# The way down of a mixture's turned block, moved between the two halves of the gate and the value products

## The chip, the cores and the metric

The kernel runs on one core of a Trainium2 chip. The metric is the device time of one execution in microseconds (us); the time before is the median of three runs.

## The reference, cut to what matters

The whole program is two transformer blocks on 256 tokens of width 1024: a convolution block and an attention block, then a second block with band attention and an RWKV mixer. Two of its layers are mixtures of experts, and only they are touched. Both compute, for every expert e, a gated product:

```python
# first mixture: 8 experts of width 3584, two for each token
y = y + gates[..., e:e + 1] * ((silu(h @ w13[e][:, :F]) * (h @ w13[e][:, F:])) @ w2[e])
# second mixture: 32 experts of width 256
h = silu(xt @ e_gate[e]) * (xt @ e_up[e])
out = out + (h * comb[:, e:e + 1]) @ e_down[e]
```

## The kernel before, in words

**Steps and units.** Each mixture gathers the tokens of every expert into 128 slots and then runs N steps. The first (m1) has 56 steps, 7 for each expert; the second (m2) has 16, two for each group of four experts. A step handles 512 hidden columns. It has two gate products (gate weights times tokens, half of the 1024 inputs each: `up(n, 0)` and `up(n, 1)`, into a gate bank), two value products (`up(n, 2)`, `up(n, 3)`, into a value bank), four transposes of the hidden block (`turn`) and two products back to width 1024 (`down`, into banks 5 and 6). Each of the six products eats one unit of weights: 1 MB, brought by two transfers of 512 KB, and 12 matmuls of 512 columns.

**The chain of one block.** ScalarE makes silu of the gate bank (line 1412). VectorE multiplies it by the value bank (`hidden`, line 1649), which needs the end of `up(n, 3)`. TensorE turns the result in the next step (`turn(n - 1)`, line 1291). ScalarE copies the turned block as its high part `mh_hi` (line 1416), VectorE makes the rest `mh_lo` (line 1654), and `down(n - 1)` (lines 1311 to 1315) needs both. After an expert's last `down` the banks 5 and 6 are emptied (lines 1422 and 1660).

**Rings.** A unit lands in `ring_raw` (6 slots). ScalarE writes its high part to `ring_hi` (line 1389) and VectorE the rest to `ring_lo` (line 1396); both rings have 3 slots. A high copy of unit i waits until TensorE has finished unit i - 3, the rest waits for the high copy, and TensorE needs both. SyncE starts the transfer of unit i once unit i - 6 has been split.

**Order.** It is written out by hand for each engine. `Moe.unit(n, what)` says which place in the list of units each product of step n has, and everything goes by this list: the transfers, the splits, and the count `unit_done`, which TensorE raises after each unit. Before, the six units that TensorE goes through from one step's start are gate 0, gate 1, value 2, value 3 of step n and the two of `down(n - 1)`; their places are base to base + 5, with base = `unit(n, 0)`. ScalarE's order in a step, with `hi(i)` for a high copy, is: hi(base+3), the copy of the turned block, hi(base+4), silu, hi(base+5) to hi(base+8). VectorE's order is: lo(base+3), the rest of the turned block, lo(base+4), lo(base+5), `hidden(n)`, lo(base+6), lo(base+7), and after an expert's end the emptying of the banks, lo(base+8).

Of the kernel before, what the change touches and what calls it, by code (L numbers as in the profile page):

```python
# [89 lines left out]
class Moe:  # L90
# [10 lines left out]

    def unit(self, n, what):

        if what < 4:
            return what if n == 0 else 6 * n - 2 + what
        return 6 * n + what + (4 if n < self.N - 1 else 0)


def col_rows():
# [13 lines left out]
def block_pair(nc, A, out, known):  # L123
# [134 lines left out]
    with ExitStack() as ctx:  # L258
# [939 lines left out]
        def moe_pe(pe, m, H, counted=None):  # L1198
# [62 lines left out]
            def halves(i):  # L1261
                eng.wait_ge(T.sem("hi_done"), SB + i + 1)
                eng.wait_ge(T.sem("lo_done"), SB + i + 1)
                s = (SB + i) % SPLIT
                return ring_hi[:, s, :], ring_lo[:, s, :]

            def finish(last, i, label):
                last.then_inc(T.sem("unit_done"), 1)
                T.mark(label, "unit_done", U + i + 1)

            def up(n, what, o):
                g, h, i = n // m.per, what % 2, m.unit(n, what)
                if m.G == 1:
                    by_k = lambda w: (lambda k: w.rearrange("p (k n) -> p k n", n=512)[:, k, :])
                else:
                    by_k = lambda w: (lambda k: w.rearrange("p (e k n) -> p e k n", e=2, k=4)[:, :, k, :])
                    o = o.rearrange("p (e n) -> p e n", e=2)
                wh, wl = (by_k(w) for w in halves(i))
                for k in range(4):
                    kk = 4 * h + k  # L1280
                    mm(o, xg_hi[:, g, kk, :], wh(k), start=(kk == 0), stop=False)  # L1281
                    mm(o, xg_lo[:, g, kk, :], wh(k), start=False, stop=False)  # L1282
                    last = mm(o, xg_hi[:, g, kk, :], wl(k), start=False, stop=(kk == KT - 1))  # L1283
                finish(last, i, f"{nm} up {n} {what}")

            def turn(n):
                eng.wait_ge(*T.at(f"{nm} hidden {n}"))
                if n:
                    eng.wait_ge(*T.at(f"{nm} turned_lo {n - 1}"))
                for k in range(4):  # L1290
                    last = nc.tensor.transpose(bank[TURN][:, k * P:(k + 1) * P], hid[n % 2][:, k * P:(k + 1) * P],  # L1291
                                               ident[:, :])
                last.then_inc(pe.tick(f"mm {nm} turn {n}"), 1)

            def down(n):
                g, first = n // m.per, n % m.per == 0
                eng.wait_ge(*T.at(f"{nm} turned_lo {n}"))
                if first and g:
                    eng.wait_ge(*T.at(f"{nm} y {g - 1}"))
                if n == 0:  # L1300
                    eng.wait_ge(*T.at(f"{nm} selT 0"))
                    eng.wait_ge(*T.at(f"{nm} selT 1"))
                for h in range(2):
                    i = m.unit(n, 4 + h)
                    wh, wl = (w.rearrange("p (k n) -> p k n", n=D) for w in halves(i))
                    for c in range(2):
                        o, ns = bank[DOWN + c][:, :], slice(512 * c, 512 * c + 512)
                        for k in range(2):
                            begin = first and h == 0 and k == 0
                            end = n % m.per == m.per - 1 and h == 1 and k == 1  # L1310
                            mm(o, mh_hi[:, 2 * h + k, :], wh[:, k, ns], start=begin, stop=False,  # L1311
                               skip_group_check=True)
                            mm(o, mh_lo[:, 2 * h + k, :], wh[:, k, ns], start=False, stop=False,  # L1313
                               skip_group_check=True)
                            last = mm(o, mh_hi[:, 2 * h + k, :], wl[:, k, ns], start=False, stop=end,  # L1315
                                      skip_group_check=True)
                    finish(last, i, f"{nm} down {n}")

            def gate_slots():
                eng.wait_ge(*T.at(f"{nm} gates"))  # L1320
                for g in range(m.NG):
                    for a in range(TT):
                        last = mm(bank[SPARE][:, g * m.G:(g + 1) * m.G], psel[:, a, g * P:(g + 1) * P].bitcast(F32),
                                  gates[:, g, a, 0:m.G], start=(a == 0), stop=(a == 1))
                last.then_inc(pe.tick(f"mm {nm} ge"), 1)

            def turn_sel(q):
                if q == 2:
                    eng.wait_ge(*T.at(f"{nm} ge"))
                if q == 3:  # L1330
                    eng.wait_ge(*T.at(f"{nm} selT 2"))
                for i in range(2):
                    for a in range(TT):
                        last = nc.tensor.transpose(bank[turn_bank[q]][:, i * S + a * P:i * S + a * P + P],
                                                   psel[:, a, (2 * q + i) * P:(2 * q + i + 1) * P].bitcast(F32),
                                                   ident[:, :])
                last.then_inc(pe.tick(f"mm {nm} selT {q}"), 1)
# [12 lines left out]
            for n in range(m.N):  # L1350
                if n >= 2:
                    eng.wait_ge(*T.at(f"{nm} silu {n - 2}"))
                up(n, 0, bank[gate_bank(n)][:, :])
                if n:
                    turn(n - 1)
                up(n, 1, bank[gate_bank(n)][:, :])
                if n >= 2:
                    eng.wait_ge(*T.at(f"{nm} hidden {n - 2}"))
                up(n, 2, bank[value_bank(n)][:, :])
                up(n, 3, bank[value_bank(n)][:, :])  # L1360
                if n == 0:
                    gate_slots()
                    turn_sel(0)
                    turn_sel(1)
                if n in (1, 2):
                    turn_sel(n + 1)
                    T.mark(f"{nm} psel read", *pe.last)
                if n:
                    down(n - 1)
            eng.wait_ge(*T.at(f"{nm} selT 3"))  # L1370
            for g in range(m.NG - 1):
                if g == m.NG - 2:
# [785 lines left out]
        def _(eng):  # L2158
# [299 lines left out]
            def last_rows():  # L2458
                turn_row(turned)
                turn_row(turned)  # L2460

            moe_pe(pe, m1, tD, last_rows)
            rest_pe(pe, m1, tD)
            ln_stats("ln3", tA, 26, 16)
# [36 lines left out]
            ln_stats("ln5", tA, 0, 16, summed=True)  # L2501
            pe.stage = "m2"
            moe_pe(pe, m2, xT)
            rest_pe(pe, m2, xT)
            ln_stats("ln6", tA, 18, 0)
# [754 lines left out]
```

## Time and profile before

| | |
|---|---|
| median of 3 runs | 2320.7 us (2320.04 to 2328.55) |
| the profiled execution's own time | 2317.63 us |
| its span | 2315.9 us |
| TensorE busy in the span | 2225.8 us |
| VectorE busy in the span | 1719.8 us |
| ScalarE busy in the span | 1378.0 us |
| steps of m1 and m2 | 56 and 16, one every 17.0 us |

The span is the profiled execution from first to last instruction; 1.7 us of its time lie around it. In the timeline each row has a start, a duration, the engine, the line, the operation, output and inputs, and in brackets how long the engine had been idle and what ended that. A matmul's duration includes its way through the array, so rows overlap; what one costs in a dense stream is the distance between starts. PEld is TensorE's load of stationary operands.

### The profile page before, as it was taken

How to read it: one execution, taken by the hardware profiler on the slowest of the kernel's cores; microseconds unless marked ns; L12 is line 12 of the kernel's file. 1: busy time of each engine (PE TensorE's matmuls, PEld its weight loads, DVE VectorE, ACT ScalarE, POOL GpSimd, SP SyncE). 2: the span in 40 equal slices, each digit the busy share in tenths (PEclk: the TensorE clock that was granted, in tenths of full speed). 3: DMA queues.
4: the chain of work that ended last, by engine and by line, in shares of the span. 5: the costliest groups of instructions: out<-in, count | busy, mean ns of one | idle time of the engine just before them, and what ended most of it. 6: DMA issues, size and time to landing. Idle time of an engine off the chain costs nothing.

```text
span 2315.9 us, 36497 instructions
## 1 busy us (share of the span) xinstructions
PE 2225.8 (96%) x14806; PEld 1910.1 (82%) x14806; DVE 1719.8 (74%) x1680; ACT 1378.0 (60%) x1296; POOL 88.3 (4%) x164
## 2 busy tenths in 40 slices
PE   7999999998999999999999999998998897999997
PEld 6778999887788888888888888887997796888887
DVE  3865444656789888888888888875586467899954
ACT  3244334545677777777777777764564335777743
POOL 7400000001000000000000000000000000000000
PEclk9999999999999999999999999999999899999999
DMA  9785754676599999999999999995640232999930
GB/s 334 231 276 185 255 184 164 205 232 200 189 344 393 376 366 376 367 376 369 372 370 372 373 368 372 370 347 41 199 143 8 93 128 92 374 369 367 375 116 19
DMA packets 339968, 618.80 MB, mean 267 GB/s; under 512 B 24813, under 2 KB 165944, under 8 KB 339800
## 3 DMA queue, kind: packets, MB, share of 16 engines
q1 hardware_dynamic: 338992, 616.13, 76.2%
q8 instruction: 121, 1.98, 0.4%
q10 hardware_dynamic: 808, 0.30, 0.1%
q14 instruction: 47, 0.39, 0.0%
HBM read 614.26 MB, written 1.05 MB: 266 GB/s over the span
## 4 chain that ended last, share of the span: by engine, by line
PE 75%; DVE 3%; ACT 2%; issue 1%; DVEq 0%; ACTq 0%
PE bank L1281 11%; PE bank L1282 11%; PE bank L1283 11%; PE bank L1313 6%; PE bank L1315 6%; PE bank L1311 6%; PE bank L2191 4%; PE bank L2192 4%; PE bank L2193 4%; PE bank L1254 1%; PE bank L1291 1%; PE bank L600 1%; PE bank L1345 1%; PE bank L2284 1%; PE bank L2275 1%
## 5 line engine op out<-in xcount | busy, mean ns | idle before, releaser
L1396 DVE TENSOR_TENSOR ring_lo<-ring_raw,ring_hi 128x2048 fp32r<-128x2048 f32 x432 | 988.2, 2291 | 137.9 <-ACT ring_hi L1389 137.5
L1389 ACT ACTIVATE ring_hi<-ring_raw 128x2048 fp32r<-128x2048 f32 x432 | 827.8, 1920 | 297.4 <-PE bank L1283 181.3
L1281 PE MATMUL bank<-ring_hi,xg_hi 128*128 128x512 f32 x1152 | 456.3, 396 | 5.8 <-DVE ring_lo L1396 3.6
L1282 PE MATMUL bank<-ring_hi,xg_lo 128*128 128x512 f32 x1152 | 449.6, 390 | 0.0
L1283 PE MATMUL bank<-ring_lo,xg_hi 128*128 128x512 f32 x1152 | 449.4, 390 | 0.0
L2191 PE MATMUL bank<-Hh,ring_hi 128*128 128x256 f32 x1032 | 298.9, 290 | 13.4 <-DVE Hl L2890 7.9
L476 DVE TENSOR_TENSOR ring_lo<-ring_raw,ring_hi 128x2048 fp32r<-128x2048 f32 (+1 forms) x96 | 217.8, 2280 | 124.7 <-ACT ring_hi L458 117.3
L2193 PE MATMUL bank<-Hh,ring_lo 128*128 128x256 f32 x1032 | 294.9, 286 | 0.0
L2192 PE MATMUL bank<-Hl,ring_hi 128*128 128x256 f32 x1000 | 286.1, 286 | 0.0
L1281 PEld LDWEIGHTS bank<-ring_hi,xg_hi 128*128 128x128 f32 x1152 | 216.4, 188 | 51.3 <-ACT ring_hi L1389 4.0
L1283 PEld LDWEIGHTS bank<-ring_lo,xg_hi 128*128 128x128 f32 x1152 | 216.3, 188 | 46.8
L1282 PEld LDWEIGHTS bank<-ring_hi,xg_lo 128*128 128x128 f32 x1152 | 216.5, 188 | 43.1
L458 ACT ACTIVATE ring_hi<-ring_raw 128x2048 fp32r<-128x2048 f32 (+1 forms) x96 | 181.6, 1899 | 79.8 <-PE bank L2193 55.0
L1311 PE MATMUL bank<-ring_hi,mh 128*128 128x512 f32 x576 | 228.4, 396 | 0.0
L1313 PE MATMUL bank<-ring_hi,mh 128*128 128x512 f32 x576 | 228.2, 396 | 0.0
L1315 PE MATMUL bank<-ring_lo,mh 128*128 128x512 f32 x576 | 228.1, 396 | 0.0
L2191 PEld LDWEIGHTS bank<-Hh,ring_hi 128*128 128x128 f32 x1032 | 201.0, 195 | 18.3 <-issue 14.0
L2193 PEld LDWEIGHTS bank<-Hh,ring_lo 128*128 128x128 f32 x1032 | 201.4, 195 | 0.0
L2192 PEld LDWEIGHTS bank<-Hl,ring_hi 128*128 128x128 f32 x1000 | 195.5, 196 | 0.1
L1315 PEld LDWEIGHTS bank<-ring_lo,mh 128*128 128x128 f32 x576 | 108.4, 188 | 26.2
L1313 PEld LDWEIGHTS bank<-ring_hi,mh 128*128 128x128 f32 x576 | 108.5, 188 | 25.8
L1311 PEld LDWEIGHTS bank<-ring_hi,mh 128*128 128x128 f32 x576 | 108.4, 188 | 25.7
(496 smaller groups left out, 2751.3 us busy)
## 6 DMA issues: line engine op xcount, KB each, us to landing
ring_raw<-in_moe_w SPq DMA_DIRECT2D x672, 512.0 KB, 5.1
ring_raw<-in_ada_w SPq DMA_DIRECT2D x96, 512.0 KB, 5.4
ring_raw<-in_ffn_w SPq DMA_DIRECT2D x66, 512.0 KB, 5.0
ring_raw<-in_exp_gate SPq DMA_DIRECT2D x64, 512.0 KB, 4.7
ring_raw<-in_exp_up SPq DMA_DIRECT2D x64, 512.0 KB, 4.8
ring_raw<-in_exp_down SPq DMA_DIRECT2D x64, 512.0 KB, 4.7
ring_raw<-in_w_in SPq DMA_DIRECT2D x42, 512.0 KB, 5.0
ring_raw<-in_conv_in_w SPq DMA_DIRECT2D x16, 512.0 KB, 8.8
```

Of the source, the lines that this page charges most:

```text
L476: nc.vector.tensor_tensor(ring_lo[:, i % SPLIT, 0:kt * c], ring_raw[:, n % RAW, 0:kt * c], ring_hi[:, i % SPLIT, 0:kt * c].bitcast(F32), A ...
L1281: mm(o, xg_hi[:, g, kk, :], wh(k), start=(kk == 0), stop=False)
L1282: mm(o, xg_lo[:, g, kk, :], wh(k), start=False, stop=False)
L1283: last = mm(o, xg_hi[:, g, kk, :], wl(k), start=False, stop=(kk == KT - 1))
L1311: mm(o, mh_hi[:, 2 * h + k, :], wh[:, k, ns], start=begin, stop=False, skip_group_check=True)
L1313: mm(o, mh_lo[:, 2 * h + k, :], wh[:, k, ns], start=False, stop=False, skip_group_check=True)
L1315: last = mm(o, mh_hi[:, 2 * h + k, :], wl[:, k, ns], start=False, stop=end, skip_group_check=True)
L1389: nc.scalar.activation(ring_hi[:, at % SPLIT, :], ring_raw[:, n % RAW, :], ACT.Copy)\
L1396: nc.vector.tensor_tensor(ring_lo[:, at % SPLIT, :], ring_raw[:, n % RAW, :], ring_hi[:, at % SPLIT, :].bitcast(F32), ALU.subtract).then_i ...
L2191: mm(o, wh[:, k, cs], Xh[:, k, :], start=(k == 0), stop=False)
L2192: mm(o, wh[:, k, cs], Xl[:, k, :], start=False, stop=False)
L2193: last = mm(o, wl[:, k, cs], Xh[:, k, :], start=False, stop=(k == kt - 1))
```

## The change

It changes the places in the list of units and moves one call. In a step the units are now gate 0, gate 1, the two of `down(n - 1)`, value 2, value 3. TensorE runs `down(n - 1)` after `up(n, 1)` and no longer after `up(n, 3)`. As transfers and splits go by the list, the units arrive and are split in the new order. The code of ScalarE and VectorE is unchanged, word for word; where it speaks of base + 4 and base + 5 these now are the value units. Step 0 and the last block's `down` keep their places. Below the change line numbers are larger by 4.

```diff
--- before.py
+++ after.py
@@ -101,9 +101,13 @@
     def unit(self, n, what):
 
+        if n == 0 and what < 4:
+            return what
+        if what < 2:
+            return 6 * n - 2 + what
         if what < 4:
-            return what if n == 0 else 6 * n - 2 + what
-        return 6 * n + what + (4 if n < self.N - 1 else 0)
+            return 6 * n + what
+        return 6 * n + what + (2 if n < self.N - 1 else 0)
@@ -1354,6 +1358,8 @@
                 if n:
                     turn(n - 1)
                 up(n, 1, bank[gate_bank(n)][:, :])
+                if n:
+                    down(n - 1)
                 if n >= 2:
                     eng.wait_ge(*T.at(f"{nm} hidden {n - 2}"))
                 up(n, 2, bank[value_bank(n)][:, :])
@@ -1365,8 +1371,6 @@
                 if n in (1, 2):
                     turn_sel(n + 1)
                     T.mark(f"{nm} psel read", *pe.last)
-                if n:
-                    down(n - 1)
```

TensorE, one step in the middle of m1, before; of each unit's 12 matmuls the first stands here, with its waits. bank1 is the gate bank, bank3 the value bank, bank4 the turned block, bank5 the way down, tC the hidden block, mh the turned copy:

```order
L1281 MATMUL bank1<-ring_hi,xg_hi_53 128x512 [waits lo_done,hi_done,act_m1]
...
L1291 MATMUL bank4<-ident,tC 128x128 [waits dve_m1]
...
L1281 MATMUL bank1<-ring_hi,xg_hi_53 128x512 [waits lo_done,hi_done]
...
L1281 MATMUL bank3<-ring_hi,xg_hi_53 128x512 [waits lo_done,hi_done,dve_m1]
...
L1281 MATMUL bank3<-ring_hi,xg_hi_53 128x512 [waits lo_done,hi_done]
...
L1311 MATMUL bank5<-ring_hi,mh 128x512 [waits lo_done,hi_done,dve_m1]
...
L1311 MATMUL bank5<-ring_hi,mh 128x512 [waits lo_done,hi_done]
```

The same step on TensorE, after:

```order
L1285 MATMUL bank1<-ring_hi,xg_hi_53 128x512 [waits lo_done,hi_done,act_m1]
...
L1295 MATMUL bank4<-ident,tC 128x128 [waits dve_m1]
...
L1285 MATMUL bank1<-ring_hi,xg_hi_53 128x512 [waits lo_done,hi_done]
...
L1315 MATMUL bank5<-ring_hi,mh 128x512 [waits lo_done,hi_done,dve_m1]
...
L1315 MATMUL bank5<-ring_hi,mh 128x512 [waits lo_done,hi_done]
...
L1285 MATMUL bank3<-ring_hi,xg_hi_53 128x512 [waits lo_done,hi_done,dve_m1]
...
L1285 MATMUL bank3<-ring_hi,xg_hi_53 128x512 [waits lo_done,hi_done]
```

The two units into bank5, whose first matmul waits for VectorE's `mh_lo`, stand one unit behind the transposes and no longer three; the two into bank3 now end the step.

VectorE, the same stretch of m1, before:

```order
L1654 TENSOR_TENSOR mh<-bank4,mh 128x512 [waits act_m1]
L1396 TENSOR_TENSOR ring_lo<-ring_raw,ring_hi 128x2048 [waits hi_done] x2
L1649 SCALAR_TENSOR_TENSOR tC<-tC,ge,bank3 128x512 [waits pe_m1,unit_done,act_m1]
L1396 TENSOR_TENSOR ring_lo<-ring_raw,ring_hi 128x2048 [waits hi_done] x4
L1654 TENSOR_TENSOR mh<-bank4,mh 128x512 [waits act_m1]
```

and after:

```order
L1658 TENSOR_TENSOR mh<-bank4,mh 128x512 [waits act_m1]
L1400 TENSOR_TENSOR ring_lo<-ring_raw,ring_hi 128x2048 [waits hi_done] x2
L1653 SCALAR_TENSOR_TENSOR tC<-tC,ge,bank3 128x512 [waits pe_m1,unit_done,act_m1]
L1400 TENSOR_TENSOR ring_lo<-ring_raw,ring_hi 128x2048 [waits hi_done] x4
L1658 TENSOR_TENSOR mh<-bank4,mh 128x512 [waits act_m1]
```

Nothing moved on VectorE, but `hidden` (line 1649, now 1653) waits for a `unit_done` that TensorE raises two units later in its step, and four rests queue behind it.

## Rows read from the trace of the kernel before

**Rows 1.** The page: span, then busy time, share and instructions of three engines.
```profile
span 2315.9 us, 36497 instructions
...
PE 2225.8 (96%) x14806; PEld 1910.1 (82%) x14806; DVE 1719.8 (74%) x1680; ACT 1378.0 (60%) x1296; POOL 88.3 (4%) x164
```

**Rows 2.** Busy times of two stretches (m1, m2): length, engines, granted clock, DMA share, GB/s.
```profile
619.50:1572.30 952.80, 952.27 (x4312) 781.69 (x4312) 829.15 (x456) 692.34 (x457) 0.71 (x2) 1.00 1.00 365
1961.00:2233.50 272.50, 272.14 (x1272) 224.89 (x1272) 233.83 (x151) 192.63 (x137) 0.00 (x0) 1.00 0.92 348
```

**Rows 3.** Timeline of TensorE in one step of m1: start, duration, line, operation.
```profile
1008.80 0.39 PE L1281 MATMUL bank<-ring_hi,xg_hi 128*128 128x512 f32 x1
...
1011.32 0.39 PE L1283 MATMUL bank<-ring_lo,xg_hi 128*128 128x512 f32 x1
1011.55 0.60 PE L1291 MATMUL bank<-ident,tC 128*128 128x128 f32 x4
1011.90 0.48 PE L1281 MATMUL bank<-ring_hi,xg_hi 128*128 128x512 f32 x1
1012.22 0.40 PE L1282 MATMUL bank<-ring_hi,xg_lo 128*128 128x512 f32 x1
...
1014.76 0.39 PE L1281 MATMUL bank<-ring_hi,xg_hi 128*128 128x512 f32 x1
...
1020.20 0.39 PE L1311 MATMUL bank<-ring_hi,mh 128*128 128x512 f32 x1
...
1025.81 0.39 PE L1281 MATMUL bank<-ring_hi,xg_hi 128*128 128x512 f32 x1
```

**Rows 4.** Timeline of ScalarE in the same step.
```profile
1011.81 1.92 ACT L1389 ACTIVATE ring_hi<-ring_raw 128x2048 fp32r<-128x2048 f32 x1 [0.83 <-PE bank L1283]
1013.63 0.58 ACT L1416 ACTIVATE mh<-bank 128x512 fp32r<-128x512 f32 x1
```

**Rows 5.** Timeline of VectorE in the same step.
```profile
1013.76 2.29 DVE L1396 TENSOR_TENSOR ring_lo<-ring_raw,ring_hi 128x2048 fp32r<-128x2048 f32 x1 [0.45 <-ACT ring_hi L1389]
1015.97 0.68 DVE L1654 TENSOR_TENSOR mh<-bank,mh 128x512 fp32r<-128x512 f32 x1
...
1021.90 0.74 DVE L1649 SCALAR_TENSOR_TENSOR tC<-tC,ge,bank 128x512 f32<-128x512 f32 x1
1022.56 2.29 DVE L1396 TENSOR_TENSOR ring_lo<-ring_raw,ring_hi 128x2048 fp32r<-128x2048 f32 x1
```

**Rows 6.** Timelines at m1's start: VectorE, then TensorE, then its weight load.
```profile
617.50 6.70 DVE L1396 TENSOR_TENSOR ring_lo<-ring_raw,ring_hi 128x2048 fp32r<-128x2048 f32 x3 [2.46 <-ACT ring_hi L1389]
...
619.95 0.47 PE L1281 MATMUL bank<-ring_hi,xg_hi 128*128 128x512 f32 x1 [1.79 <-DVE ring_lo L1396]
620.25 0.39 PE L1282 MATMUL bank<-ring_hi,xg_lo 128*128 128x512 f32 x1
...
619.91 0.19 PEld L1281 LDWEIGHTS bank<-ring_hi,xg_hi 128*128 128x128 f32 x1 [2.00 <-ACT ring_hi L1389]
```

**Rows 7.** Timeline of VectorE in m2: the hidden block, and the emptied banks.
```profile
2062.70 1.28 DVE L1660 TENSOR_TENSOR xg_lo<-bank,xg_hi 128x512 fp32r<-128x512 f32 x2
...
2074.16 0.87 DVE L1649 SCALAR_TENSOR_TENSOR tC<-tC,ge,bank 128x256 f32<-128x256 f32 x2
2074.95 2.29 DVE L1396 TENSOR_TENSOR ring_lo<-ring_raw,ring_hi 128x2048 fp32r<-128x2048 f32 x1
```

**Rows 8.** Waits: engine, line, what was waited for, us in total, times, longest.
```profile
ACT ring_hi L1389 <- PE bank L1283: 181.3, 262, 2.3
...
ACT ring_hi L1389 <- PE bank L1315: 108.4, 124, 1.2
```

**Rows 9.** Timeline of TensorE: matmuls that follow an idle gap, in several stages.
```profile
432.64 0.36 PE L2191 MATMUL bank<-Hh,ring_hi 128*128 128x256 f32 x1 [2.40 <-DVE ring_lo L476]
...
581.83 3.42 PE L1254 MATMUL bank<-psel,ring_hi 128*128 128x512 f32 x8 [2.00 <-ACT xT L2758]
...
1574.23 0.39 PE L1345 MATMUL bank<-pselT,xg_hi 128*128 128x256 f32 x1 [2.01 <-DVE xg_lo L1660]
...
2235.43 0.39 PE L1345 MATMUL bank<-pselT,xg_hi 128*128 128x256 f32 x1 [2.01 <-DVE xg_lo L1660]
```

**Rows 10.** Busy times of the two stretches around the gap at 1574 us.
```profile
1572.00:1576.00 4.00, 1.99 (x10) 1.77 (x10) 1.29 (x2) 1.68 (x3) 0.00 (x0) 0.82 0.00 0
1576.00:1580.00 4.00, 4.00 (x30) 4.00 (x29) 2.83 (x3) 3.93 (x3) 0.00 (x0) 0.75 0.05 7
```

## The prediction, made before the changed kernel ran

> **What bounds the kernel now.** I read the page first, for which engine is nearly full: TensorE, 2225.8 of 2315.9 us [rows 1]. Then the busy times of the two stretches that the change touches: in m1 TensorE is busy for 952.27 of 952.80 us, in m2 for 272.14 of 272.50, both at the full granted clock [rows 2]. So both stretches last exactly as long as TensorE's work, and a reordering of that work can gain nothing there. It can only open gaps. The timeline gives the step: from one step's first matmul to the next 1025.81 - 1008.80 = 17.01 us, without a gap [rows 3]. The starts give its parts: gate unit 2.75, four transposes 0.35, second gate unit 2.86 (its first matmul takes 0.32 and not 0.23, the pipeline being refilled), the two value units 5.44, the two units down 5.61. ScalarE, which paces VectorE, waits in these stretches for TensorE to free a ring slot [rows 8], so the other engines have slack, and the question is how much slack each dependence has.
>
> **The change, part by part.**
>
> *Work.* No instruction is added or removed, and each unit keeps its bytes and its splits. The transfers, already listed in the order of use, stay so. Cost nothing; what covers them is the ring of 6 slots, and they get more time if the steps get longer.
>
> *First dependence: the turned block.* `down(n - 1)` needs `mh_lo`. After the first gate unit's slot ends (1011.55) the high copy of the next unit starts at 1011.81, the copy of the turned block, queued behind it, at 1013.63 [rows 4], the rest of that unit at 1013.76 and `mh_lo` at 1015.97, 0.68 long [rows 5]: it ends 5.10 after the gate unit. From VectorE's end to TensorE's next matmul the nearest row shows 0.16: the first of three rests that began at 617.50 ended 2.29 later, and the matmul came at 619.95 [rows 5, 6]. So `down` can start at 5.26. Before, it came at 1020.20, 8.65 after that point, with 3.4 to spare. Now it would come 0.35 + 2.86 = 3.21 after it. TensorE waits 5.26 - 3.21 = **2.05 us**, and refills for 0.07 (the first matmul at 619.95 takes 0.30 instead of 0.23 [rows 6]). With nothing else late, 2.12 a step. ScalarE's high copy and VectorE's rest of unit base+3 stand ahead of the turned block in both queues, and neither can be passed.
>
> *Second dependence: the hidden block.* `hidden(n)` waits for `up(n, 3)`. Before, that ended two units ahead of the step's end, and `hidden` and the rest of the next unit (base + 6) hid under `down`, 5.61 us. Now `up(n, 3)` is the step's last unit. VectorE sits in `hidden`'s wait, and behind it in its queue is lo(base + 6), which the next step's first matmul needs. The price from the end of the last slot: the last matmul's modelled end is 0.16 behind its slot (1011.32 + 0.39 against 1011.55) and the waiting engine starts 0.10 after that [rows 3, 4]; `hidden` to the next rest 0.65 (1021.90 to 1022.56); the rest 2.29 [rows 5]; and 0.16 to TensorE. In all **3.36 us**, with the refill 3.43. In m2 `hidden` is two instructions and takes 0.79 instead of 0.65 [rows 7]: 3.57. This price does not shrink with time: the ring's high part is ready long before, but the queue's order is fixed. Value products and all copies behind have their inputs: counting on from `mh_lo` with the same durations, lo(base + 4) ends 3.3 us before the first value unit begins and lo(base + 5) 1.0 us before the second.
>
> *How often.* The turned wait comes once in each step but the first, 55 + 15. The hidden wait comes between steps 1 and 2 up to the last: 54 + 14 (behind step 0 stand other works; behind the last the scatter, which does not need it). After an expert's end VectorE also empties two banks (1.28 us [rows 7]) between two rests; of it 0.35 reaches `mh_lo`, because VectorE, done with lo(base + 8), would idle for 0.85 before the next rest. That is 7 + 7 times, 5 us.
>
> *Sum without the clock.* m1: 54 x 3.43 + 55 x 2.12 = 302. m2: 14 x 3.57 + 15 x 2.12 = 82. Banks 5. Together **+389 us**, a step of 22.6 us.
>
> *The clock.* The trace of before has no such gap inside the steps, so this is bounded from both sides. [...] A matmul of 512 columns takes 3.42 / 8 = 0.43 there [rows 9] and 0.23 at the full clock, so 3.4 us hold 8 instead of 15: a fall costs up to 1.6 us. The hidden gap will show 3.2 us of idle (3.36 less the 0.16 of modelled end), longer than any that did not fall; I take 0.85 of them. A late part of the slow stretch falls into the second gate unit, whose delay the turned wait swallows, so 1.3 us each: 68 x 0.85 x 1.3 = 75. The turned gap will show 1.9 us, between 1.79 (no) and 2.0 (mostly yes); I take a quarter, 70 x 0.25 x 1.6 = 28. Bounds: 0 if it never falls, and 138 x 1.6 = 221 if always. I take **+103**.
>
> [...] The load for the matmul at 619.95 started at 619.91, after the wait and not ahead of it [rows 6]. [...]
>
> **Sum:** 2317.6 (profiled execution) + 389 + 103 = 2809. The median of before is 3.1 above its profiled execution, so **2812 us**.
>
> **The rivals.**
>
> *The clock stays up.* Both waits as priced, no fall: 2317.6 + 389 + 3 = 2709. For it: two of seven long gaps had no fall, and the stream is otherwise dense. Against: the other five. 0.2.
>
> *The clock falls after nearly every gap.* 2317.6 + 389 + 221 + 3 = 2931. [...] Against: a slow gate unit shortens the wait behind it. 0.13. [...]
>
> *Only one wait counts.* If the turned wait were hidden (ScalarE's turned copy ready sooner than rows 4 say), 54 x 3.43 + 14 x 3.57 + 3 gives 2556. Against: the queue order. 0.05.
>
> *Not slower.* The true pace of these stretches could be the transfers': the DMA share is 1.00 at 365 GB/s in m1 [rows 2], and a TensorE row's end is modelled. Then gaps would take time that is lost anyway as long as they stay below the waits for transfers, and the time would stay 2320.7. It decides only if ScalarE's copies waited for landings; they waited for TensorE, 181.3 + 108.4 us [rows 8]. That the change does not do what it says (VectorE's rest not in fact behind `hidden`) would give the same time; the order of instructions excludes it. 0.02 together.
>
> **How the numbers follow.** Forecast 0.6 (2760 to 2865), clock up 0.2, clock always down 0.13, one wait 0.05, not slower 0.02. The range 2700 to 2900 holds the forecast and the clock-up case; 0.2 lie outside. A measurement of this kernel can tell about 0.5%, 12 us, from no change; faster 0.01, same 0.01, slower 0.98.
>
> **What would show it.** Steps of m1 every 22.6 to 24.5 us instead of 17.0. TensorE's first gate matmul idle for about 3.2 us, released by `ring_lo`, 68 times, some 220 us. The first matmul down idle for about 1.9 us, released by `mh`, 70 times, some 132 us. `hidden` waiting for the last value matmul. A granted clock of 0.8 to 0.95 in m1; a DMA share near 0.72. The work outside m1 and m2 unchanged. I am wrong in the first step if `hidden` is not late, in the second if the turned gap is short, and in the clock's term if the mean clock stays 1.00 or falls below 0.75.

## The result and the profile after

The changed kernel takes 2835.4 us (2833.3 to 2839.6, four runs) against 2320.4 us for the kernel before: 1.220 times as long, 95% interval 1.217 to 1.223, or 515 us more. The forecast was 2812 us in a range of 2700 to 2900.

The page of the changed kernel has the same number of instructions. Span, busy times and the granted clock in 40 slices:

```profile
span 2835.7 us, 36497 instructions
...
PE 2396.0 (84%) x14806; PEld 1996.2 (70%) x14806; DVE 1714.8 (60%) x1680; ACT 1374.6 (48%) x1296; POOL 87.8 (3%) x164
...
PEclk9999999998999999998999898999999999999899
```

VectorE and ScalarE do the work of before [rows 1] in 520 us more. TensorE's busy time rose by 170 us without one more matmul, so its matmuls themselves became slower (not by all of the 170 us: by an estimate, 138 x (0.16 + 0.07) = 32 of them are the modelled ends and the refills at the gaps). The two stretches that answer to [rows 2], first m1, then m2 (length, busy times, granted clock, DMA share, GB/s):

```profile
620.70:1972.90 1352.20, 1084.05 (x4312) 848.52 (x4312) 824.17 (x455) 689.76 (x456) 0.39 (x2) 0.92 0.76 257
2364.50:2753.10 388.60, 313.12 (x1272) 247.11 (x1272) 233.33 (x150) 191.43 (x136) 0.00 (x0) 0.90 0.67 244
```

m1 is 399 us longer and m2 116 us, together the whole difference. TensorE is idle for 268 and 75 us in them, where it had half a microsecond each, and the clock is no longer full. The waits of the changed kernel name who was late (us in total, times, longest):

```profile
DVE tC L1653 <- PE bank L1287: 284.5, 70, 4.4
...
PE bank L1285 <- DVE ring_lo L1400: 229.2, 70, 4.9
...
PE bank L1315 <- DVE mh L1658: 117.9, 70, 2.2
```

The first line is VectorE sitting in `hidden` until the last value unit is done; before, that line had no wait of note. The second and third are TensorE waiting for the rest queued behind `hidden`, and for the turned block. One step of m1 on TensorE, the gaps in brackets:

```profile
1011.47 0.47 PE L1285 MATMUL bank<-ring_hi,xg_hi 128*128 128x512 f32 x1 [3.19 <-DVE ring_lo L1400]
...
1013.48 0.63 PE L1285 MATMUL bank<-ring_hi,xg_hi 128*128 128x512 f32 x1
1013.91 0.63 PE L1286 MATMUL bank<-ring_hi,xg_lo 128*128 128x512 f32 x1
...
1021.05 0.50 PE L1315 MATMUL bank<-ring_hi,mh 128*128 128x512 f32 x1 [1.78 <-DVE mh L1658]
...
1037.13 0.77 PE L1285 MATMUL bank<-ring_hi,xg_hi 128*128 128x512 f32 x1 [3.19 <-DVE ring_lo L1400]
```

and on VectorE:

```profile
1008.38 0.75 DVE L1653 SCALAR_TENSOR_TENSOR tC<-tC,ge,bank 128x512 f32<-128x512 f32 x1 [4.04 <-PE bank L1287]
1009.04 6.69 DVE L1400 TENSOR_TENSOR ring_lo<-ring_raw,ring_hi 128x2048 fp32r<-128x2048 f32 x3
1018.11 2.29 DVE L1400 TENSOR_TENSOR ring_lo<-ring_raw,ring_hi 128x2048 fp32r<-128x2048 f32 x1 [2.38 <-ACT ring_hi L1393]
1020.32 0.68 DVE L1658 TENSOR_TENSOR mh<-bank,mh 128x512 fp32r<-128x512 f32 x1
```

The reader is to see the step of [rows 3 to 5] pulled apart. `hidden` starts when the value unit ends, three rests stand behind it, and the first of them ends at 1011.33, 0.14 ahead of TensorE's matmul. That step's first unit then has starts 0.43 apart (1013.48 to 1013.91) where [rows 3] have 0.23: the granted clock was 0.50 of full speed from 1013.0 to 1015.5 us.

### The profile page after: what moved, and what is told of

It is laid out like the page before. It is cut to its first block, busy times and chain, and to the rows that moved or that the text cites. A ratio compares the mean times of both kernels' runs of the same rounds, so it can differ in the third digit from the quotient of the medians.

```text
span 2835.7 us, 36497 instructions
## 1 busy us (share of the span) xinstructions
PE 2396.0 (84%) x14806; PEld 1996.2 (70%) x14806; DVE 1714.8 (60%) x1680; ACT 1374.6 (48%) x1296; POOL 87.8 (3%) x164
## 4 chain that ended last, share of the span: by engine, by line
PE 59%; DVE 18%; ACT 6%; issue 2%; DVEq 0%; ACTq 0%
DVE ring_lo L1400 12%; PE bank L1285 8%; PE bank L1287 8%; PE bank L1286 8%; PE bank L1315 6%; PE bank L1317 5%; PE bank L1319 5%; ACT ring_hi L1393 5%; PE bank L2195 3%; PE bank L2196 3%; PE bank L2197 3%; DVE tC L1653 2%; DVE mh L1658 2%; PE bank L1258 1%; PE bank L1349 1%
## 5 line engine op out<-in xcount | busy, mean ns | idle before, releaser
L1285 PE MATMUL bank<-ring_hi,xg_hi 128*128 128x512 f32 x1152 | 498.7, 433 | 231.3 <-DVE ring_lo L1400 229.2
L1287 PE MATMUL bank<-ring_lo,xg_hi 128*128 128x512 f32 x1152 | 489.3, 425 | 0.0
L1286 PE MATMUL bank<-ring_hi,xg_lo 128*128 128x512 f32 x1152 | 487.1, 423 | 0.0
L1285 PEld LDWEIGHTS bank<-ring_hi,xg_hi 128*128 128x128 f32 x1152 | 234.6, 204 | 306.2 <-issue 246.8
L1315 PE MATMUL bank<-ring_hi,mh 128*128 128x512 f32 x576 | 248.9, 432 | 117.9 <-DVE mh L1658 117.9
L1287 PEld LDWEIGHTS bank<-ring_lo,xg_hi 128*128 128x128 f32 x1152 | 238.2, 207 | 55.8
L1286 PEld LDWEIGHTS bank<-ring_hi,xg_lo 128*128 128x128 f32 x1152 | 237.7, 206 | 48.0
L1317 PE MATMUL bank<-ring_hi,mh 128*128 128x512 f32 x576 | 241.1, 419 | 0.0
L1319 PE MATMUL bank<-ring_lo,mh 128*128 128x512 f32 x576 | 240.7, 418 | 0.0
L1315 PEld LDWEIGHTS bank<-ring_hi,mh 128*128 128x128 f32 x576 | 116.1, 202 | 173.3 <-DVE mh L1658 147.5
L1653 DVE SCALAR_TENSOR_TENSOR tC<-tC,ge,bank 128x512 f32<-128x512 f32 (+1 forms) x88 | 55.8, 649 | 284.6 <-PE bank L1287 284.5
```

## The experiments

All are edits of the changed kernel. The two disputed points are which wait carries the loss, and how much is the clock.

### One rest ahead of `hidden`

```diff
-                hidden(n)
-                for i in range(6, 9):
+                lo(base + 6)
+                hidden(n)
+                for i in range(7, 9):
```

> The changed kernel, but VectorE makes the rest of unit base + 6 ahead of `hidden(n)` and not behind it; nothing else. Theory (two waits, each priced from the queue's order, plus a clock term): the idle of 3.2 us ahead of the first gate matmul goes. What is late next: after `hidden`, lo(base + 7) ends about 0.3 us after the second gate unit could begin, and the turned block's rest comes about 0.3 later than in the changed kernel, so about 2.45 us a step stay, 70 x 2.45 = 172, and with fewer falls of the clock some 20 to 60 more: 2490 to 2570 us. Rival (the turned wait and the clock are the main cost, the hidden wait runs beside them): over 2650 us.

Measured: 2600.3 us, 1.120 times the kernel before (1.117 to 1.123). The rival is out; the hidden wait is a large cost of its own. The time lies above the theory's range. TensorE's gaps, in an ordinary step and in the one after an expert's end:

```profile
1358.05 0.80 PE L1315 MATMUL bank<-ring_hi,mh 128*128 128x512 f32 x1 [3.11 <-DVE mh L1658]
...
1378.95 0.50 PE L1315 MATMUL bank<-ring_hi,mh 128*128 128x512 f32 x1 [1.93 <-DVE mh L1658]
1398.39 0.50 PE L1315 MATMUL bank<-ring_hi,mh 128*128 128x512 f32 x1 [1.91 <-DVE mh L1658]
```

The last two are 19.44 us apart, a step of 17.01 and 2.43: the price of 2.45 was right. Three things were missed. After an expert's end the emptied banks now reach the turned block nearly in full (3.1 instead of 1.9 us, 13 times, 16 us). Four gaps of 4.90 us ahead of the gate matmul, in steps 1 and 2 of each mixture, are still there, 20 us; the part on both edits says where they come from. And the clock fell in 43 of 70 steps after the gap ahead of the way down (counted as those where the following matmuls' starts lie over 0.37 us apart): 9 times after the 13 gaps of 3.1 us, 34 times after the other 57, of mostly 1.9 us. A step with a fall took 20.98 us, 1.54 more. With 47 falls in all the sum is 172 + 16 + 20 + 72 = 280 us, which is what was measured over the kernel before in the same runs.

### The turned copies first

First ScalarE's order, then VectorE's:

```diff
-                hi(base + 3)
                 if n:
                     turned(n - 1)
+                hi(base + 3)
+                if n:
                     hi(base + 4)
...
+                if n:
+                    turned(n - 1)
                 lo(base + 3)
...
-                turned(n - 1)
```

> The changed kernel, but ScalarE's high copy and VectorE's rest of the turned block stand ahead of the high copy and the rest of unit base + 3; nothing else. Theory: the turned block's rest ends about 2 us sooner than `down` can begin, so that wait goes; the hidden wait stays at 3.36 and 3.5 us, 54 x 3.43 + 14 x 3.57 = 235, 7 more in four steps in which the turned lists of places stand behind the value products, and the clock's falls after the long gaps, up to 1.6 us each because no later wait swallows a part: 80 to 110. 2640 to 2675 us. Rival (only the turned wait counts): under 2450 us.

Measured: 2592.3 us, 1.117 times (1.113 to 1.120). The wait for the turned block is gone from the list of waits, and the hidden wait stays as priced. But the time is 48 us under the theory's range: in m1's steps 3 to 54 the clock did not fall. A stretch of m1 (length, busy times, granted clock, DMA share, GB/s):

```profile
700.00:1500.00 800.00, 675.62 (x2972) 540.60 (x2972) 584.81 (x324) 492.19 (x326) 0.00 (x0) 1.00 0.87 308
```

One of its gaps on TensorE, and the matmul behind it, whose start follows 0.31 later, at the full clock:

```profile
1034.57 0.47 PE L1285 MATMUL bank<-ring_hi,xg_hi 128*128 128x512 f32 x1 [3.19 <-DVE ring_lo L1400]
1034.88 0.40 PE L1286 MATMUL bank<-ring_hi,xg_lo 128*128 128x512 f32 x1
```

52 such gaps in a row, 51 of them of 3.19 us and one of 3.56, one every 20.44 us (20.65 after an expert's end), and after none of them the clock fell. In m2, where the gap is 3.31 us and a step without a fall 20.6, it fell after 9 of 12. In the changed kernel gaps of the same 3.19 us were mostly followed by a fall, so a gap's length alone doesn't settle it. The second execution of this kernel has a mean granted clock of 0.971 against 0.975 and took 6 us longer: a few more falls, but nearly the same picture.

### Both

The kernel `both_first` has both edits above; `both_two` has a second rest, lo(base + 7), ahead of `hidden` as well.

> The changed kernel with both moves: the rest of unit base + 6 ahead of `hidden(n)`, and the copies of the turned block ahead of unit base + 3. Theory: both waits go, but lo(base + 7), now behind `hidden`, ends 0.26 us after the second gate unit could begin: 70 x 0.3 = 18 to 25 us over the kernel before, 2335 to 2350 us, at the full clock. Rival (the new place of the way down costs by itself, through the transfers, the banks or the ring of three slots): over 2400 us.

Measured: 2388.8 us, 1.029 times (1.026 to 1.032), 44 us over the expectation's range.

> As the one before, but the rests of both units base + 6 and base + 7 stand ahead of `hidden(n)`. Theory: no wait is left in the steps; the time is the kernel's of before, 2310 to 2325 us. Rival (the new place costs by itself): over 2400 us. If the new place of the way down brings something of its own, it shows here as a time under 2310.

Measured: 2363.1 us, 1.020 times (1.016 to 1.024). Between the two lie 26 us, about as priced for the late lo(base + 7); but 43 us over the kernel before were left, which neither theory had. In the steady steps of `both_two` there is next to nothing: from 700 to 1500 us TensorE is busy 797.14 us at the full clock. The gaps stand in steps 1 and 2. TensorE, then ScalarE, of `both_two`:

```profile
656.82 0.60 PE L1338 MATMUL bank<-ident,psel 128*128 128x128 f32 x4
662.32 0.77 PE L1285 MATMUL bank<-ring_hi,xg_hi 128*128 128x512 f32 x1 [4.90 <-DVE ring_lo L1400]
...
657.46 0.60 ACT L1431 ACTIVATE pselT<-bank 128x512 fp32r<-128x512 f32 x1 [6.73 <-PE bank L1338]
657.95 5.50 ACT L1393 ACTIVATE ring_hi<-ring_raw 128x2048 fp32r<-128x2048 f32 x3
```

In steps 1 and 2 TensorE turns a list of places (line 1338) after the last value unit. ScalarE's copy of it stands ahead of the high copy of base + 6, so that high copy too now waits for the end of TensorE's step. Before, the way down came behind and covered this.

### The lists of places ahead of the value units

The kernel `both_lists` is `both_two` with this edit as well:

```diff
                 if n:
                     down(n - 1)
+                if n in (1, 2):
+                    turn_sel(n + 1)
+                    T.mark(f"{nm} psel read", *pe.last)
...
-                if n in (1, 2):
-                    turn_sel(n + 1)
-                    T.mark(f"{nm} psel read", *pe.last)
```

> The changed kernel with the turned copies first and two rests ahead of `hidden`, as in the run at 2363 us, and in addition the turned lists of places in steps 1 and 2 of each mixture stand ahead of the value units and not behind them. Theory: the 43 us that were left over the kernel before are four gaps of 4.9 us and their falls, because ScalarE's next high copy stands behind the copy of these lists; without them the time is the one before, 2315 to 2325 us. Rival (something in the steady steps costs): 2350 us or more.

Measured: 2337.5 us against 2325.3 in the same runs, 1.005 times (1.003 to 1.007). The gaps of 4.90 us are gone, and steady steps last 17.0 us as before. 12 us are left. 10.5 of them are in the steps after an expert's end, 7 in m1 that take 17.69 and 7 in m2 that take 17.81 us. VectorE, then TensorE, in one:

```profile
741.13 1.28 DVE L1665 TENSOR_TENSOR xg_lo<-bank,xg_hi 128x512 fp32r<-128x512 f32 x2
742.33 2.29 DVE L1400 TENSOR_TENSOR ring_lo<-ring_raw,ring_hi 128x2048 fp32r<-128x2048 f32 x1
744.52 0.69 DVE L1659 TENSOR_TENSOR mh<-bank,mh 128x512 fp32r<-128x512 f32 x1
...
745.27 0.50 PE L1315 MATMUL bank<-ring_hi,mh 128*128 128x512 f32 x1 [0.42 <-DVE mh L1659]
```

The emptied banks push the turned block's rest past the point where the way down wants it. So the new place costs nothing in an ordinary step once the other engines' orders follow it, and it brings nothing either. No version here beats the kernel before.

### The gaps filled with matmuls

```diff
+            def fill(n, count):
+                if n == 4:
+                    eng.wait_ge(*T.at(f"{nm} selT 3"))
+                if 4 <= n < m.N - 1:
+                    for _ in range(count):
+                        mm(bank[SPARE][:, :], xg_hi[:, m.NG - 1, 0, :],
+                           xg_hi[:, m.NG - 1, 0:4, :].rearrange("p k s -> p (k s)"), start=True, stop=True)
...
+                fill(n, 7)
                 if n:
                     down(n - 1)
...
+                fill(n, 13)
```

`fill(n, 13)` ends the step, behind `up(n, 3)`. The kernel `filled` has both calls, `filled_hidden` only this last one. The added matmuls' results are not used.

> The changed kernel with matmuls that compute nothing needed, put where TensorE would idle: 7 of 512 columns ahead of the way down (1.6 us) and 13 behind the last value unit (3.0 us), in steps 4 to 54 of m1 and 4 to 14 of m2. They write to a bank that is free there, and no wait is touched. Theory (the two waits are paced by VectorE, and the rest of the loss is the lower clock after the gaps): the waits stay as long, the clock stays up, so steps of 22.5 us: 2317.6 + 389 + 7 for the lists of places + about 10 for falls in the first steps: 2715 to 2735 us. Rival (the clock is no term of its own, the waits are longer than priced): 2835 us or more, since the added work comes on top.

Measured: 2733.6 us, 1.176 times (1.172 to 1.180). 1240 matmuls of 512 columns are added (20 in each of 62 steps), and the time falls by 102 us. The place of the long gap on TensorE:

```profile
1011.60 3.11 PE L1359 MATMUL bank<-xg_hi 128*128 128x512 f32 x13
1014.95 0.47 PE L1285 MATMUL bank<-ring_hi,xg_hi 128*128 128x512 f32 x1 [0.24 <-DVE ring_lo L1410]
```

Its stretch of m1:

```profile
700.00:1500.00 800.00, 782.40 (x3401) 620.96 (x3401) 531.66 (x294) 445.75 (x294) 0.00 (x0) 1.00 0.80 280
```

The slot before the 13 matmuls ends at 1011.60 and the next step begins at 1014.95: 3.35 us, the hidden wait, priced at 3.36. The step is 22.53 us, the sum's 22.6, and the clock is 1.00. Outside the first steps this takes the clock's term away and nothing else: 102 us by the medians, 107 us when each kernel is taken against the kernel before of its own runs.

> As the one before, but only the 13 matmuls in the gap ahead of the next step are put in; the 1.9 us gap ahead of the way down stays empty. Theory (a fall is tied to a gap's place in time as much as to its length): the falls of the long gaps go, those of the short ones come in about half of the steps, as in the kernel with the rest first, whose gaps of 1.93 us had a fall in 43 of 70: 2720 + 35 x 1.5 = 2750 to 2790 us. Rival (only gaps of 3 us let the clock fall): 2720 us.

Measured: 2810.4 us, 1.209 times (1.206 to 1.213), above the theory's range. In the filled steps only the short gap is left open. After 55 of the 70 short gaps (1.79 or 1.81 us of idle in most, 1.45 to 2.15 in all) the clock fell; in the changed kernel it fell after 21 of the same 70. Its stretch of m1:

```profile
700.00:1500.00 800.00, 729.53 (x2981) 575.51 (x2980) 502.19 (x279) 422.60 (x279) 0.00 (x0) 0.94 0.76 265
```

The mechanism of the expectation held, its count of 35 did not; its 43 of 70 from `rest_first` were also not all gaps of 1.93 us. The long gaps' falls are gone, but with 34 more after the short ones the time is just 25 us below the changed kernel's.

### The step made longer, the gap unchanged

The kernel `turned_longer` is the one with the turned copies first, and eight such matmuls in each of 62 steps:

```diff
+                fill(n, 8)
                 up(n, 3, bank[value_bank(n)][:, :])
```

> The kernel with the turned copies first (2592 us, steps of 20.44 us, a 3.19 us gap in each and no fall of the clock for 49 steps on end), with 8 matmuls of 512 columns that compute nothing needed put between the two value units of 62 steps: 1.82 us more dense work a step, the gap untouched. Theory (whether a gap lets the clock fall depends on where in time it lies, and the step's length sets whether that place moves from step to step): falls return in most steps, 2592 + 113 + 50 to 100 = 2755 to 2805 us. Rival (gap length alone decides, and 3.2 us without a second gap never does it): 2592 + 113 = 2705 us.

Measured: 2776.4 us, 1.195 times (1.191 to 1.199). The added matmuls are 113 us, the time rose by 184. One of its gaps with what follows:

```profile
1041.34 0.47 PE L1285 MATMUL bank<-ring_hi,xg_hi 128*128 128x512 f32 x1 [3.19 <-DVE ring_lo L1409]
...
1042.41 0.63 PE L1285 MATMUL bank<-ring_hi,xg_hi 128*128 128x512 f32 x1
1042.84 0.63 PE L1286 MATMUL bank<-ring_hi,xg_lo 128*128 128x512 f32 x1
```

and the stretch:

```profile
700.00:1500.00 800.00, 691.57 (x2810) 551.79 (x2809) 505.79 (x278) 420.22 (x277) 0.00 (x0) 0.93 0.74 264
```

The gap is the same 3.19 us as in the kernel with the turned copies first, ahead of the same work, and now the clock falls after 65 of 70, in the steps of m1 with the plain hidden gap after 50 of 52 where it was 0 of 52 before. What the edit changed is 1.82 us of matmuls in the middle of the step: the gaps came 22.25 us apart where there was no fall, instead of 20.44. Each fall then stretched the step to 23.86. The rival (length alone decides) is out.

The trace of this kernel also shows a place in time that shifts while gap and work stay the same. The clock fell after 44 gaps in a row, from 707 to 1733 us. The fall began 0.06 us before the next matmul at first, a little later in each step, and at last 1.45 us behind it. The next gap, ahead of the matmul at 1757.04, was as long and led into the same work, and no fall came; one step later the fall began 0.27 us before the matmul. The stretches behind these two gaps, the last with a fall and the one without (length, busy times, granted clock, DMA share, GB/s):

```profile
1734.00:1738.50 4.50, 4.50 (x16) 3.66 (x15) 3.45 (x2) 0.24 (x1) 0.00 (x0) 0.62 0.96 321
1757.00:1761.00 4.00, 3.96 (x20) 3.34 (x21) 4.00 (x2) 0.52 (x2) 0.00 (x0) 1.00 0.72 229
```

## Why the prediction was right, point by point

**TensorE bounds both stretches, and reordering can only open gaps.** Right: all 515 us lie there, as idle time of TensorE and as slower matmuls, and `both_lists` shows that the new place itself brings nothing.

**The hidden wait.** Priced at 3.36 us a step, 3.2 of them shown as idle; the trace of after shows 3.19 in m1 and 3.31 or 3.32 in m2, and `filled` 3.35 from slot to slot. It was read from four durations of [rows 3 to 6], and none was off. The count was right too, with one miss: in four steps, 1 and 2 of each mixture, the idle is 4.90. The step of the prediction that added up the hidden wait took the high copy of base + 6 for ready; there it stands behind the copy of the list of places. 4 x 1.7 = 7 us. `both_lists`, where these gaps are gone, shows the cause.

**The turned wait.** Priced at 2.12 with refill; 1.79 to 1.81 of idle are shown after a unit at full clock, 0.08 less than the 1.89 forecast. Where the first gate unit ran in part at half the clock it shrinks, down to 1.37 (ahead of 1456.88, granted clock 0.50 from 1449.2 to 1452.6 us), as the clause on the swallowed part says. `turned_first` shows that the order of two queues was all there was to it.

**The emptied banks.** 0.35 us forecast; in `filled` the steps of m1 after an expert's end last 22.81 to 22.88 us and the others 22.51 to 22.56, some 0.3 more.

**The weight load and the refill.** 0.07 a gap for the refill stand in the sum. In `turned_first` the load for the matmul at 1034.57 started at 1034.54, after the wait again, and the next matmul came 0.31 later instead of 0.23: 0.08.

**The clock.** Forecast +103 us, from 58 falls after long gaps at 1.3 us and 17.5 after short ones at 1.6. No run shows these two prices as such; they were the author's estimate. What the runs show of a fall is a granted clock of 0.50, in before for 3.4 us (1574.6 to 1578.0, behind the gap at 1574.23 [rows 9]), and a step that is longer by 1.54 us in `rest_first`, 1.56 in `filled_hidden` and 1.61 in `turned_longer`. The trace of after has 61 and 21 falls. `filled` takes away 102 us with 69 of these 82, 1.48 each, and keeps 13, in steps that aren't filled, some 19 us by an estimate at the same 1.48: the term was about 121. With the 107 us that are taken against the kernel before of the same runs it is 1.55 each and 127 in all. The sum then closes within 8 us of the 515: 389 + 7 + 121 = 517, or 523.

This term was right partly by luck. The prediction drew single chances, by the length of a gap, from gaps elsewhere in the trace of before: of seven of 2.0 to 2.6 us five were followed by a stretch at 0.50, and those ahead of 432.64 and 1585.77 were not (1.00 in the 3.4 us behind each). The runs show that these aren't chances of each gap: in m1 of one kernel 0 of 52 gaps let the clock fall, in m1 of another 50 of the same 52. Had the turned wait been absent, the same reasoning would have put the clock's term 50 to 80 us too high: the expectation of `turned_first` did so, with 80 to 110 us where 2589.1 (its profiled execution) - 2317.6 - 235 - 7 leaves 30. In the changed kernel the steps are 22.5 to 26.5 us long and uneven, and the falls spread over gaps of both kinds, so that the mean came out.

**The rivals.** The clock stays up (2709): out by the 102 us of `filled`, whose own time is near it. The clock falls after nearly every gap (2931): out for this kernel, with falls after 82 of 140 gaps. In m1 it nearly holds for `turned_longer` (50 of 52 gaps), and with the same gap it doesn't for `turned_first` (0 of 52). Only one wait counts (2556): out by `rest_first` and `turned_first`, each of which takes off 235 to 243 us. Not slower: out.

## What to carry to other kernels

Where several engines each follow an order written by hand, moving a call on one of them moves what its completions release on the others. Ask for every wait in the other queues which event it now means, and what is queued behind it: here the code of VectorE was unchanged, but its wait came two units later, with the next unit's split behind it. If a reordering is wanted for another reason, move the copies and splits with it (2835 to 2337 us here, the lists of places included), and look at the odd steps, the first and the last of a group, by themselves.

## What the runs showed of the hardware that was not expected

Whether the granted clock fell to 0.50 after an idle gap of TensorE did not hang on the gap's length alone. Gaps of 3.19 us in m1, every 20.44 us: 0 of 52. The same gaps with 1.82 us more work in the step, 22.25 us apart without a fall and 23.86 with one: 50 of 52. Gaps of mostly 1.8 us, alone in steps of 22.5 us without a fall and 24.06 with one: 55 of 70. In `turned_first` steps that differ by 0.14 us and gaps that differ by 0.12 (m1 and m2) went from 0 of 52 to 9 of 12. So `turned_first`, with its regular beat, was in luck for a whole stretch (granted clock 1.00 from 700 to 1500 us), and an edit that looks harmless ended that (0.93 in `turned_longer`): 1.8 us more in a step (9%) cost 70 us here beyond the added work, which no wait shows.

Matmuls that compute nothing, put where TensorE must wait anyway, made the changed kernel 102 us faster. In the kernel before there are no such gaps in the steps, so it gains nothing there.

What stays open: what exactly in the place of a gap decides. The slow slide in `turned_longer`, with its one gap without a fall, speaks for the place in time, but no run here moved a gap in time without changing the step's length or the work in it.
